# A transformer prefix on one Trainium2 core: the first block's residual kept channel-major

## The reference

```python
def rms_norm(x, g):
    y = xf * lax.rsqrt(jnp.mean(xf * xf, axis=-1, keepdims=True) + RMS_EPS)
    return y * g
def first_block(x, ...):
    h = h + short_conv_mixer(rms_norm(h, conv_norm_g), conv_w_in, conv_w, conv_w_out)
    h = h + swiglu_ffn(rms_norm(h, conv_ffn_norm_g), conv_ffn_w13, conv_ffn_w2)
    h = h + mla_mixer(rms_norm(h, mla_norm_g), ...)       # keys and values from rms_norm(h, kv_norm_g)
    h = h + swiglu_ffn(rms_norm(h, mla_ffn_norm_g), ...)
# short_conv_mixer: gate_b, gate_c, val = split(x @ w_in); (gate_b * conv3(gate_c * val)) @ w_out
# swiglu_ffn: g, u = split(x @ w13); (silu(g) * u) @ w2       (D_FF is 2816)
```

## Time and profile before

| | |
|---|---|
| median of three runs | 1596.67 us |
| the profiled execution's own time | 1596.24 us |
| its span, first to last instruction | 1594.4 us |
| mean granted TensorE clock | 0.935 of full |
| PE busy | 1301.5 us (82%) |
| VectorE, ScalarE, POOL busy | 540.8, 444.9, 60.9 us |
| bytes moved | 519.39 MB |
| chain that ended last | DMA 49%, PE 45%, VectorE 3%, ScalarE 2% |

### The profile page before, as it was taken

One profiled execution on the slowest core, in us unless ns is written; L12 is line 12 of the kernel. 1 busy time (PEld: TensorE's weight loads), 2 busy tenths in 40 slices (PEclk: granted clock), 3 DMA queues, 4 the chain that ended last, 5 costly groups with the idle time before them and its releaser, 6 DMA issues.

```text
span 1594.4 us, 29664 instructions
## 1 busy us (share of the span) xinstructions
PE 1301.5 (82%) x12728; PEld 973.2 (61%) x12728; DVE 540.8 (34%) x911; ACT 444.9 (28%) x760; POOL 60.9 (4%) x84
## 2 busy tenths in 40 slices
PE   8999999999999999999676677666666667677666
PEld 8989999878999987876344344334333334334333
DVE  6666555776655578641000101001010010010001
ACT  5454444655444457522011011011011011011011
POOL 3000000001000025000000000000000000000000
PEclk9999999999999999999889889989998889879887
DMA  9555554444555536499999999999999999999997
GB/s 354 202 183 185 184 196 152 155 156 138 193 184 204 181 124 261 190 425 428 431 431 432 431 432 432 432 431 431 432 430 432 432 431 432 431 432 432 432 431 308
DMA packets 46214, 519.39 MB, mean 326 GB/s; under 512 B 5583, under 2 KB 5844, under 8 KB 8660
## 3 DMA queue, kind: packets, MB, share of 16 engines
q1 hardware_dynamic: 44928, 517.34, 79.5%
q0 software_dynamic: 896, 0.99, 0.3%
q10 hardware_dynamic: 340, 0.35, 0.1%
HBM read 517.61 MB, written 1.05 MB: 325 GB/s over the span
## 4 chain that ended last, share of the span: by engine, by line
DMA 49%; PE 45%; DVE 3%; ACT 2%; issue 1%; SPq 0%; POOL 0%; ACTq 0%; POOLq 0%; DVEq 0%
DMA work<-in_moe_units 48%; PE ps L317 11%; PE ps L319 11%; PE ps L318 11%; PE ps L2260 5%; PE ps L2251 1%; PE ps L990 1%; PE ps L989 0%; ACT w_split L276 0%; PE ps L484 0%; DVE xT_lo L564 0%; DVE w_split L280 0%; PE ps L1691 0%; DMA work<-in_conv_w 0%; PE ps L2294 0%
## 5 line engine op out<-in xcount | busy, mean ns | idle before, releaser
L2251 PE MATMUL ps<-ring,work 128*32 128x256 f32 x2976 | 202.9, 419 | 91.6 <-DMA ring<-in_moe_units 91.6
L2466 DVE TENSOR_TENSOR work<-ps,work 128x128 f32<-128x128 f32 x64 | 18.7, 292 | 738.8 <-ACT work L2379 738.8
L317 PE MATMUL ps<-xT_hi,w_split 128*128 128x256 f32 x960 | 266.5, 278 | 1.4 <-DVE xT_lo L564 1.4
L318 PE MATMUL ps<-xT_lo,w_split 128*128 128x256 f32 x960 | 265.4, 276 | 0.0
L319 PE MATMUL ps<-xT_hi,w_split 128*128 128x256 f32 x960 | 265.3, 276 | 0.0
L280 DVE TENSOR_TENSOR w_split<-ring,w_split 128x2048 fp32r<-128x2048 f32 (+3 forms) x101 | 227.9, 2259 | 92.4 <-ACT w_split L276 91.2
L276 ACT ACTIVATE w_split<-ring 128x2048 fp32r<-128x2048 f32 (+3 forms) x105 | 196.3, 1872 | 143.4 <-PE ps L319 143.3
L2251 PEld LDWEIGHTS ps<-ring,work 128*32 128x32 f32 x2976 | 95.3, 118 | 189.4 <-DMA ring<-in_moe_units 118.5
L317 PEld LDWEIGHTS ps<-xT_hi,w_split 128*128 128x128 f32 x960 | 180.2, 188 | 3.6 <-issue 2.5
L318 PEld LDWEIGHTS ps<-xT_lo,w_split 128*128 128x128 f32 x960 | 180.4, 188 | 0.9
L319 PEld LDWEIGHTS ps<-xT_hi,w_split 128*128 128x128 f32 x960 | 180.3, 188 | 0.0
(11 more groups left out here) (372 smaller groups left out, 1566.8 us busy)
## 6 DMA issues: line engine op xcount, KB each, us to landing
ring<-in_moe_units SPq DMA_DIRECT2D x124, 2048.0 KB, 26.8
ring<-in_ffn_units SPq DMA_DIRECT2D x66, 1024.0 KB, 4.8
x_slots<-in_moe_units SPq DMA_DIRECT2D x32, 2048.0 KB, 25.7
work<-in_moe_units SPq DMA_DIRECT2D x32, 2048.0 KB, 26.9
ring<-in_conv_units SPq DMA_DIRECT2D x15, 1024.0 KB, 11.8
ring<-in_win_units SPq DMA_DIRECT2D x9, 1024.0 KB, 4.8
ring<-in_wo_units SPq DMA_DIRECT2D x4, 1024.0 KB, 4.9
kept_slot<-in_moe_units SPq DMA_DIRECT2D x2, 2048.0 KB, 14.7
```

The source lines that it names most:

```text
L317: pe.matmul(out_ap, stat_hi, mov_hi, start=first, stop=False, skip_group_check=True)
L318: pe.matmul(out_ap, stat_hi, mov_lo, start=False, stop=False, skip_group_check=True)
L2251: last = pe.matmul(ps[CAP * j:CAP * j + CAP, b, 0:BLK], xstat[:, 4 * half + k, CAP * lane:CAP * lane + CAP], w[k][:, j // 2, BLK * (j % 2) ...
L2466: dve.tensor_tensor(astat[par], bank(b, 256).rearrange("p (c s j m) -> p c s j m", c=2, s=2, j=2)[:, :, 1, :, :], wk(SI, 128).rearrange("p ...
```

## The change

- The host also gives x transposed (`x_turned`, 128 x 8 x 256) and all gain vectors as columns (`columns`). SP loads x in four pairs of channel chunks, between the two halves of the first weight unit; ScalarE loads the columns in two transfers. The 15 row loads, the two parameter transposes and the 16 input transposes go, and the constants are loaded behind the second weight unit.
- The residual of the first block is `hT`, channel-major. The projections back to the width become `by_output`: weights stationary, 48 matmuls of 256 columns, for the convolution output, the first w2 and the attention output. The second w2 stays by_token; ahead of it PE transposes `hT` back (16 blocks, `rows_of_tokens`) and ScalarE copies them to `h`.
- The residual is added by pairs of chunks (`turned_lo`), the operands are made from `hT` directly, and `by_pair` starts a stage on the first pair.
- The norm's sum of squares: ScalarE squares `hT` (4 x 128x512), VectorE adds them in three steps (`tree`), PE sums over partitions with a matrix of ones. For the convolution and both feed-forward stages that gives the sum of each token on every partition, 128x256 (`sum_rows_pe`, `mean_rows_dve`), and POOL raises those 128x256 to the power -0.5 (`rstd_rows_pool`). For attention it gives 128x2 as before (`sum_columns_pe`).
- In the convolution the factor is applied behind the products: its square to the gate (`RB_SQ`, made by POOL) and itself behind the taps.

```diff
+    hT = kept_slot[:, 0, :].rearrange("p (k t) -> p k t", k=KD)
...
+    def by_output(pe, u, x, ks, first=False, last_unit=False, i=None, chunks=range(KD)):
+
+        unit_ready(pe, u, i)
+        hi, lo = weights(u, 2, D)
+        for c in chunks:
+            cs = slice(c * P, c * P + P)
+            for q, k in enumerate(ks):
+                last = passes(pe, bank(4 + c // 2, T, (c % 2) * T), hi[:, q, cs], lo[:, q, cs], x[0][:, k, :], x[1][:, k, :],
+                              first and q == 0 and c % 2 == 0, False)
+            if last_unit and c % 2 and c < KD - 1:
+                last.then_inc(s("all_acc"), 1)
+        return last
...
+    def by_pair(pe, u, out_bank, x, ready, halves=False):
...
+        for b in range(KD // 2):
+            if halves and b == KD // 4:
+                unit_ready(pe, u)
+            pe.wait_ge(*mark(ready, b + 1))
+            for f in range(2):
+                for k in (2 * b, 2 * b + 1):
+                    last = passes(pe, bank(out_bank, T, f * T), hi[:, k, f * P:(f + 1) * P], lo[:, k, f * P:(f + 1) * P],
+                                  x[0][:, k, :], x[1][:, k, :], f == k == 0, k == KD - 1)
         last.then_inc(s("used"), 1)
...
+    def squares(act, prev, tag):
+        for b in range(4):
+            if prev is None:
+                act.wait_ge(s(f"x_loaded{b}"), 16)
+            else:
+                act.wait_ge(*mark(f"{prev}_h", b + 1))
+            last = act.activation(wk(SQT + 512 * b, 512), hT[:, 2 * b:2 * b + 2, :].rearrange("p k t -> p (k t)"), ACT.Square)
+        last.then_inc(s("all_sq"), 1)
+    def tree(dve, tag):
+        dve.wait_ge(*mark(f"{tag}_sq", 1))
+        dve_step(dve, dve.tensor_tensor(wk(SQT, 1024), wk(SQT, 1024), wk(SQT + 1024, 1024), ALU.add))
+        dve_step(dve, dve.tensor_tensor(wk(SQT, 512), wk(SQT, 512), wk(SQT + 512, 512), ALU.add))
+        dve.tensor_tensor(wk(TREE, T), wk(SQT, T), wk(SQT + T, T), ALU.add).then_inc(s("all_tree"), 1)
+    TREE = 3072
+    def sum_rows_pe(pe, tag, b):
+        pe.wait_ge(*mark(f"{tag}_tree", 1))
+        pe.matmul(bank(b, T), const("ones"), wk(TREE, T), start=True, stop=True, skip_group_check=True).then_inc(s("all_sum"), 1)
+    def sum_columns_pe(pe, tag, b):
+        pe.wait_ge(*mark(f"{tag}_tree", 1))
+        for tt in range(TT):
+            last = pe.matmul(bank(b, 1, tt), wk(TREE + P * tt, P), const("ones")[:, 0:1], start=tt == 0, stop=True, skip_group_check=True)
+        last.then_inc(s("all_sum"), 1)
+    def mean_rows_dve(dve, tag, b):
+        dve.wait_ge(*mark(f"{tag}_sum", 1))
+        dve.tensor_scalar(rb[:, :], bank(b, T), 1.0 / D, EPS, ALU.mult, ALU.add).then_inc(s("all_mean"), 1)
+    RB_SQ = 7168
+    def rstd_rows_pool(pool, tag, squared=False):
+        pool.wait_ge(*mark(f"{tag}_mean", 1))
+        last = pool.tensor_tensor(rb[:, :], rb[:, :], const("half")[:, 0:1].broadcast_to([P, T]), ALU.pow)
+        if squared:
+            last.then_inc(s("cv_rstd"), 1)
+            pool.wait_ge(s("cv_rstd"), 1)
+            last = pool.tensor_tensor(wk(RB_SQ, T), rb[:, :], rb[:, :], ALU.mult)
+        last.then_inc(s("all_rb"), 1)
...
+    def turned_hi(act, prev, tag, gain, dst):
+        for b in range(4):
+            act.wait_ge(*mark(f"{prev}_h", b + 1))
+            for k in (2 * b, 2 * b + 1):
+                last = operand_hi(act, tag, k, gain, dst)
+            last.then_inc(s("all_hi"), 1)
+    def turned_lo(dve, units_done, prev, tag, gain, dst, split):
+        def add(b):
+            if b < 3:
+                dve.wait_ge(*mark(f"{prev}_acc", b + 1))
+            else:
+                dve.wait_ge(s("used"), units_done)
+            x = hT[:, 2 * b:2 * b + 2, :].rearrange("p k t -> p (k t)")
+            dve.tensor_tensor(x, x, bank(4 + b), ALU.add).then_inc(s("all_h"), 1)
+        lo_half(dve, split, 0)
+        add(0)
+        for b in range(1, 4):
+            add(b)
+            operand_lo(dve, tag, b - 1, gain, dst)
+        operand_lo(dve, tag, 3, gain, dst)
+        lo_half(dve, split, 1).then_inc(s("raw_read"), 1)
...
     def conv_pe(pe):
-        norm_pe(pe, "cv")
-        pe.wait_ge(s("pcol"), 1)
         clear_acc(pe)
-        keep_busy(pe, 2, 4)
         for j in range(JC):
             u = conv_first_unit(j)
             for q in range(3):
-                if q == 0 and j == ROWS_AT + 1:
-                    pe.wait_ge(s("pcol"), 2)
+                if q == 0 and j == 1:
+                    pe.wait_ge(*mark("cv_mean", 1))
                 if q == 0 and j >= 2:
                     pe.wait_ge(s("cv_y"), 2 * j - 2)
                 if q == 1 and j:
                     pe.wait_ge(s("cv_c"), j)
                 if q == 2 and j:
                     pe.wait_ge(s("cv_z"), j)
-                by_channel(pe, u + q, conv_bank(j, q), xT, ready="cvx_lo" if j == q == 0 else None, halves=j == q == 0)
-            if j == 0:
-                pe.wait_ge(s("consts_loaded"), 16)
-            if j == ROWS_AT:
-                parameter_columns(pe, 1, conv_bank(j + 1, 0))
+                if q == 2 and j == 0:
+                    pe.wait_ge(s("consts_loaded"), 16)
+                    sum_rows_pe(pe, "cv", SUM_BANK)
+                if j == q == 0:
+                    by_pair(pe, u, conv_bank(j, q), xT, "cvx_lo", halves=True)
+                else:
+                    by_channel(pe, u + q, conv_bank(j, q), xT)
             if j:
                 conv_out(pe, j - 1, u + 3)
         conv_out(pe, JC - 1, U_CONV + N_CONV - 1)
...
+        act.wait_ge(s("pcol_first"), 16)
+        for b in range(4):
+            act.wait_ge(s(f"x_loaded{b}"), 16)
+            for k in (2 * b, 2 * b + 1):
+                last = operand_hi(act, "cvx", k, lambda k: col("conv_norm", k), xT)
+            last.then_inc(s("all_hi"), 1)
+            if b % 2 == 0:
+                first_hi(act, b // 2)
+        split_hi(act, 1, size[1])
+        squares(act, None, "cv")
...
+        dve.wait_ge(s("pcol_first"), 16)
+        for b in range(4):
+            operand_lo(dve, "cvx", b, lambda k: col("conv_norm", k), xT)
+            if b % 2 == 0:
+                first_lo(dve, b // 2)
+        split_lo(dve, 1, size[1])
+        tree(dve, "cv")
+        split_lo(dve, 2, size[2])
...
             dve.wait_ge(s("cv_c"), j + 1)
+            dve.wait_ge(*mark("cv_rb", 1))
+            both = lambda at: wk(at, 512).rearrange("p (f t) -> p f t", f=2)
+            dve_step(dve, dve.tensor_tensor(both(CV), both(CV), wk(RB_SQ, T)[:, None, :].broadcast_to([P, 2, T]), ALU.mult))
...
+            t_both = wk(CV + 1536, 2048).rearrange("p (f n) -> p f n", f=2)[:, :, 0:T]
+            dve_step(dve, dve.tensor_tensor(t_both, t_both, rb2(2), ALU.mult))
...
+    def rows_of_tokens(pe):
+        pe.wait_ge(*mark("mla_h", 4))
+        for b in range(4):
+            for q in range(4):
+                last = pe.transpose(bank(4 + b, P, P * q), hT[:, 4 * (b % 2) + q, P * (b // 2):P * (b // 2) + P], ident)
+            last.then_inc(s("h_turned"), 1)
+    def rows_of_tokens_act(act):
+        for b in range(4):
+            act.wait_ge(s("h_turned"), b + 1)
+            act.activation(h[:, b // 2, 512 * (b % 2):512 * (b % 2) + 512], bank(4 + b), ACT.Copy).then_inc(s("h_rows"), 1)
...
+            by_channel(pe, u, 2 * parity, xT, i)
+            pe.wait_ge(*mark(f"{t}_mean", 1))
             by_channel(pe, u + 1, 2 * parity + 1, xT, i)
...
+            if n == 1:
+                last = by_output(pe, u, x, [0, 1], last_unit=last_block, i=i)
+            else:
+                last = by_token(pe, u, ACC, x, [0, 1], 2, D, 512, False, last_block, i=i,
+                                between=first_rows(pe, "ffn2", "n1") if last_block else None)
...
-        up(base, 0, ready=f"{t}x_lo")
+        by_pair(pe, base, 0, xT, f"{t}x_lo")
+        if n == 1:
+            clear_acc(pe, prev)
+        else:
+            rows_of_tokens(pe)
+        by_channel(pe, base + 1, 1, xT)
+        sum_rows_pe(pe, t, SUM_BANK)
+        if n == 2:
+            pe.wait_ge(s("h_rows"), 4)
+            clear_acc(pe)
...
-        add_sums(dve, base, prev, base + 1)
-        operand_dve(dve, f"{t}x", NORM_BANKS, gain, xT)
-        both_rstd_dve(dve, t)
-        rstd_rows_dve(dve, t, 4)
+        turned_lo(dve, base, prev, f"{t}x", gain, xT, base + 1)
+        tree(dve, t)
         ahead_lo(dve, base - 1)
-        rstd_rows_out(dve, t, RB_BANK)
-        dve.wait_ge(s("rb"), rb_turns[t])
...
+        mean_rows_dve(dve, t, SUM_BANK)
+        dve.wait_ge(*mark(f"{t}_rb", 1))
...
+        sum_columns_pe(pe, "mla", 0)
         latents(0)
...
+        turned_lo(dve, u, "ffn1", "mlaq", lambda k: col("mla_norm", k), xT, u + 1)
         ahead_lo(dve, u - 1)
-        operand_dve(dve, "mlax", NORM_BANKS, lambda k: col("kv_norm", k), xT)
-        both_rstd_dve(dve, "mla")
+        for b in range(4):
+            operand_lo(dve, "mlax", b, lambda k: col("kv_norm", k), xS)
+        tree(dve, "mla")
+        both_rstd_dve(dve, "mla", 0)
         ahead_lo(dve, u)
```

(19 more changed lines are left out.)

236 lines of the change are left out of this document (79 added, 157 removed), and 7 rows, old and new, of the table stages.

## The result

The changed kernel takes 1719.51 us, the median of four runs (1718.72 to 1723.62), against 1596.69 us for the kernel before: a ratio of 1.0773, 95% interval 1.0760 to 1.0786. It is 123 us slower. The profiled execution took 1719.12 us with a span of 1717.3, which is 122.9 us longer than the span before; the mean granted TensorE clock is 0.903 of full.

What follows compares the result with a forecast made beforehand. PE was taken to bound the dense stretch and bandwidth the expert stretch. Convolution +41.7, feed-forward +33.4 and +39.8, and attention +0.7 sum to +115.6 us on 1596.24: 1712 us, range 1685 to 1740.

Steps and rivals of the forecast that it cites:

- The step on which it turned: POOL's norm power over 256 columns in convolution and both feed-forward stages: 41.4 us each, bounds 37 to 46.
- The rule: Skill page: GpSimd tensor_tensor about 2.6 cycles an element, so 0.55 us for 256 columns and the change a gain.
- The clock behind a stall: PE restarts at half clock after each of three stalls, in convolution and both feed-forward stages: +1.5 us each.
- Attention: Attention's entry loses transposes (-3.4) but sums delay PE's latents: net +1.0, four units -0.3, so +0.7 us.
- The entry to the first feed-forward stage: Transposes and the gap to the first product go, pairs being added and split under PE's work: -3.8 us.
- The entry to the second feed-forward stage: The same shortening of the entry was claimed for the second feed-forward stage: -3.8 us.
- The new shape of a projection: Down units turned from by_token to by_channel shape: -0.15 us each, 11 units in the first feed-forward stage, -1.6 us.
- The rope tables beside the chain: Second feed-forward stage: POOL's rope tables slow VectorE's split from 2.29 to 4.87 us, +2.6 us.
- The head: Start of the kernel: PE starts near 8.2 us, U3 ends 2.8 us earlier, worth nothing while the power holds U4.
- The bending: Rival: POOL's wide power bends partly, say to 10 us; +17.5 us, 1614 us; chance 5%.
- the dearer power: Rival: POOL's powers cost more than the rows say; 46 us each gives 1727 us, or beyond the range; chance 4%.
- The cheap power: Rival: POOL's wide power costs only the multiplication's 1.26 us, stalls vanish; -6.2 us, 1590 us; chance 11%.

Runs made afterwards that it cites:

- e3: Kernel before plus eight idle-time POOL instructions: powers of 2 to 256 columns, one on 16 partitions, and a 256-column multiplication; 1596.67 us.
- e1: Changed kernel with POOL's three 128x256 powers replaced by multiplications by one; 1599.16 us, ratio 1.0011.
- e2: Changed kernel, powers kept, with matmuls on zeros keeping PE busy through the three waits; 1713.52 us, ratio 1.0730.
- e8: e7 with convolution sums, factor spread and U3's split reordered, and one tile of attention's second latent unit ahead of the transposes; 1589.65 us, ratio 0.9954.
- e6: e4 with attention's squares added before the preceding unit's split and the mean taken after two pairs of low parts; 1597.93 us, ratio 1.0001.
- e7: e6 plus a busier PE start, early ScalarE table load, and whole weight splits after the residual sums at stage entries; 1595.47 us, ratio 0.9989.
- e4: Changed kernel, channel-major residual kept, factor made on two columns and spread as before, in the convolution ahead of POOL's loads; 1599.44 us, ratio 1.0013.

## Why the prediction came out as it did

**Right in sign, place and size.** The forecast was 1712 us within 1685 to 1740; the measured time is 1719.5. The step on which it turned was the power: 41.4 us by the slope of the earlier trace rows, 41.2 measured, three times. The extrapolation from 20 to 256 columns held, and e3 shows the forms between, within 1.4 us of the line from 32 columns on. POOL was to begin at 26.2 and began at 26.21, and that is luck to about a microsecond: the constants came at 13.77 and not at 13.2, and the gap in the loads was 6.40 us and not 7.23; in e1 and e2, with the same work ahead of it, POOL begins at 27.32 and 27.57. U4 was to start at 76.1 and started at 75.37; the waits were to be 37.3 us in the feed-forward stages and were 36.60 and 36.48. The cover of two units and the chain behind the power, VectorE's queued split at its end, were sized right. POOL was busy 179.2 us against some 185. The expert stage kept its pace of 431 GB/s and shifted one to one but for about a microsecond. Of the last 1.8 us of the table 0.5 are there when POOL makes its first power of one column ahead of the experts (684.75 us before, 806.30 after); the other 1.3 arise in the expert stage, where POOL stands idle for 901.40 us against 900.03, and 899.46 to 901.31 us in e1 to e8. That is the spread of single executions.

**The rule and the trace.** The multiplication of 256 columns took 0.61 us behind the power and 0.62 in e1, the power 41.2, 67 times as much. The Trainium skill (GPSIMD Engine Reference, Elementwise, side-by-side cycle accounting) gives tensor_tensor about 2.6 cycles an element, by which the prediction's estimate was 0.55 us. The measured multiplication comes near to that; for a power the measurement decides, and it is far off.

**The terms that were mis-sized.**
- *The clock behind a stall*, 1.5 us each: it was 2.25, 2.26 and 2.90, so 7.4 and not 4.5 in all. The price was read off a group of 32 matmuls behind a short wait, 3.46 us long, so it could not show more than such a group holds. Behind these stalls PE's matmuls kept the pace of half clock for 4.6, 4.6 and 6.4 us; e2 shows that it was the clock, since the units took 5.56, 5.44 and 5.50 us once PE had been kept busy ahead of them.
- *Attention*, +0.7: it was about +3.4. The wait itself was in the prediction's figures: with the mean 12.8 us behind the last product and PE done with its queries at 8.3, PE is without work for some 4.5 us, which less the 3.4 of transposes gives about the +1.0. The trace has 4.05. What the sum left out stands around it. The mean came 14.4 us behind the last product and not 12.8, and the clock, for which nothing was charged here, was at 0.50 from 378 to 382 us: the first latent unit took 5.59 us (379.35 to 384.94), in e6, without its wait, 3.77. e6 shows what the wait hangs on, since it goes when VectorE's tree and mean are moved ahead.
- *The entry to the first feed-forward stage*, -3.8: it was about -2.0, with a wait of 1.36 us where "no wait there longer than 1 us" stood. The text had VectorE add pair 0 while PE runs the last pairs, and left out what stands ahead of it in VectorE's own queue. The trace shows half a split there (timeline of VectorE in the kernel after), and in e7, where it is moved, the wait is down to 0.23 us:

```profile
141.71 1.22 DVE L291 TENSOR_TENSOR w_split<-ring,w_split 128x1024 fp32r<-128x1024 f32 x1
142.84 1.28 DVE L573 TENSOR_TENSOR kept_slot<-kept_slot,ps 128x512 f32<-128x512 f32 x2
144.50 0.88 DVE L554 SCALAR_TENSOR_TENSOR xT_lo<-kept_slot,pcol,xT_hi 128x256 fp32r<-128x256 f32 x2 [0.38 <-ACT xT_hi L548]
```

- *The entry to the second feed-forward stage*, -3.8 as well: by the same reading (3.4 less its wait of 0.45) it was about -2.9.
- *The new shape of a projection*, -0.15 us a unit: a block of three units takes 16.32 us instead of 16.40, so -0.08. The by_token unit of the earlier trace rows took 5.60 us; in the loop one takes 5.50 (127.79 to 133.29 us in the kernel before).
- *The rope tables beside the chain*, +2.6: about +0.3. The splits at 521.95 and 524.81 us took 2.34 and 2.38 us, not the 4.87 of the earlier trace rows:

```profile
521.95 2.34 DVE L284 TENSOR_TENSOR w_split<-ring,w_split 128x2048 fp32r<-128x2048 f32 x1
```

- *The head*: the first product came at 9.52 us, not 8.2. ScalarE loaded a table for 1.28 us only after x had landed, and the first products ran at half clock. U3 ended at 34.62 us and not at 32.5. This cost nothing here, since the power held U4. It also made a hit of the first stall: by the prediction's own 76.1 and 32.5 it would have been 43.6 us long, where "about 40" was written and 40.75 measured.

```profile
5.06 1.28 ACT L548 ACT_TABLE_LOAD   x1 [5.06 <-DMA kept_slot<-in_x_turned]
```

**The sum.** Measured less forecast: clock +2.9, attention +2.7, entry +1.8, tail +1.8, units +0.7; against them the rope tables -2.3, U4 -0.6 and the two feed-forward waits -1.5 (0.7 and 0.8). That is +5.5 of the 7.3; the entry to the second feed-forward stage adds 0.9, and the last 0.9 us stay open. Misses of 10.8 us one way and 4.4 the other stand behind the 7.3, so the total is nearer than its terms. Two slips of arithmetic are small: 3.584 + 236 x 0.16 is 41.3, and three powers of 46 us give 1726.

**The rivals.** The bending and the dearer power fell with e3. The cheap power was rightly the less likely one, but its price was wrong: not 1590 but 1599, by e1. U4 came where its ledger had it (35.90 us against 36.0), but the ledger held the estimates for attention and the two entries that were too kind, and no half clock behind the waits, 1.7 us of it at U4. The break-even of 5.2 us for a power was therefore wrong too: with a free power the change is no gain. It becomes one only with the order of e8.

## What to carry to other kernels

Count a POOL power by its columns, not by its elements: keep the tokens on partitions for it (two columns, 0.7 us) and spread the result over columns afterwards, even at the price of a diagonal and a matmul. When a stage's data layout changes, read each in-order queue that the new sums pass through, since what the layout saves comes back as waits behind unrelated work there; e4 to e8 differ only in such order and in the start, and span 10 us. And a stall costs its own length and then the half clock behind it, here another 2.3 to 2.9 us behind stalls of 36 to 41 us and 1.7 behind one of 2.30.
